# Expert stage of a decoder trunk: token rows scattered to slots and block results fetched back through DRAM

## The chip, the cores and the metric

One core of a Trainium2 chip runs the whole kernel. It has TensorE (matrix products into PSUM), VectorE, ScalarE, GpSimd and SyncE, and 16 DMA engines that move data between DRAM and SBUF. The metric is the device time in microseconds; the figure for a kernel is the median of its runs. Profiles come from one execution.

## The reference, cut to what matters

Two layers over 256 tokens of width 1024. The change concerns the last part: a mixture of 8 SwiGLU experts, two per token, then the gated residual add and the final RMSNorm.

```python
logits = (hf @ router_w + router_b).astype(jnp.float32)
probs = jax.nn.softmax(logits, axis=-1)
top_p, top_i = lax.top_k(probs, TOP_K)            # TOP_K = 2
top_p = top_p / jnp.sum(top_p, axis=-1, keepdims=True)
...
for e in range(N_EXPERTS):                         # 8
    out = out + gates[:, e:e + 1] * _swiglu(hf, w_gate[e], w_up[e], w_down[e])   # 1024 -> 3584 -> 1024
...
x = x + gate_from_c * out                          # adaLN: shift, scale and gate come from c
return _rmsnorm_f32(x, final_norm_g)
```

Everything is float32.

## The kernel before

**Order of the work.** Attention and convolution, the dense feed-forward, the state-space layer and its GLU, the router, and then the expert stage. The activations lie with channels on the partitions and tokens along the free dimension (`buf_b` is `B`, the residual `x`; `H` the normed input).

**Blocks and slots.** Each token takes two slots, one for each expert chosen. Slots are grouped in blocks of 32 (`BLK`); an expert has at least two blocks (`LEAST`) and the whole at most 28 (`MOST`, 896 slots). In this run there are 22: 2, 6, 3, 2, 2, 2, 3 and 2 for experts 0 to 7. The router's counts give `items`, the running number of blocks, which every engine loads into registers as `upto`. VectorE works out `slot_of[0]` and `slot_of[1]`, the two slots of each token.

**Gather.** A group of 128 slots (four blocks) is gathered by matrix products: `sel` holds, for each token and slot, 1 where the slot is the token's, and `gather(g)` (L724) multiplies the token-major copy `h_tm` of `H` with it. ScalarE copies the result into `hg` (`take_gathered`). `GATHER_AT` says before which expert a group is gathered in round 0: groups 0 and 1 before expert 0, 2 and 3 before expert 1, 4, 5 and 6 before experts 2, 4 and 6.

**Rounds.** The hidden width of 3584 is cut in 7 rounds (`ROUNDS`) of 512. Within a round the experts come in order, and within an expert its blocks. GpSimd copies a block's columns into `hbuf` (L1602); TensorE makes gate and up (`gate_up`, L744: 32 products) into PSUM, ScalarE the SiLU (L1010), VectorE the product and the transpose (L1052, L1470); TensorE makes the down product of the block before (`e_down`, L753: 16 products) between two blocks' gate and up; VectorE adds it to `acc` (`keep`). Each product is two instructions in the trace.

**Weights.** Each expert and round takes three pairs of ring slots of 2 MiB (`expert_stream`; two for gate and up, one for down), 168 in all. SyncE issues them in order. Seven pair slots lie in the ring; two more (`more`) join at pair 24 (`MORE_AT`), since until then `more` holds `h_tm`, `sel`, `places` and `spread`. A pair's load waits until the last block that uses its slot is done.

**Scatter and end.** In the last round the finished block goes through `keep_last` and `gate_rows` (three VectorE operations that make the block's row of gate weights per token from `reps`) and `scatter` (L762: 8 products over four row groups), which adds it into PSUM over all tokens. `spread_turn` (L734) and the copy into `reps` prepare that in round 0. After the last block: `residual`, then the final norm by channel: squares on ScalarE, `sums` (L417) on TensorE, root, reciprocal, eight products on VectorE, four stores of `out` (L1037) from ScalarE's queue.

## Time and profile before

| what | value |
|---|---|
| runs shown | 1510.95 us median of 3 (1510.21 to 1512.93) |
| span of the profiled execution | 1512.1 us, slowest (only) core |
| TensorE, VectorE, ScalarE, GpSimd busy | 1430.2, 370.1, 159.2, 137.5 us |
| mean granted TensorE clock | 0.985 |
| DRAM traffic | 478.10 MB read, 13.63 MB written |
| expert stage | from 606.5 us to the end of the span |

The profiled execution's own time is given as its span, 1.15 us above the median of the runs. An engine's busy time is the time in which at least one of its instructions runs; a matmul's end is modelled, so a busy TensorE needn't be at its peak. In the slices each digit or number stands for a fortieth of the span, 37.8 us. In a row of the timeline the first number is the start and the second the time that the merged instructions take; what stands in brackets is how long the engine was idle before and what released it.

### The profile page before, as it was taken

The page shows a single profiled execution, that of the slowest core. Times are in us where ns is not written, and L with a number is a line of the kernel's source. Part 1 is how long each engine was busy: PE and PEld are TensorE (multiplying, and loading weights), DVE is VectorE, ACT ScalarE, POOL GpSimd, SP SyncE. Part 2 cuts the span into 40 slices and gives each one's busy share as a digit, 9 for nine tenths or more (in the row PEclk, how much of TensorE's full clock was granted, in tenths as well). Part 3 has the DMA queues.
Part 4 walks back from the last instruction along what each step waited for, and adds up shares of the span by engine and source line. Part 5 has one row for each costly group of instructions (what it writes and reads, how often), then busy time and mean ns, then how long its engine had stood idle before and what let it go on. Part 6 is the DMA issues. An engine that isn't in the chain of part 4 may idle for free.

```text
span 1512.1 us, 44722 instructions
## 1 busy us (share of the span) xinstructions
PE 1430.2 (95%) x19890; PEld 1062.4 (70%) x19890; DVE 370.1 (24%) x1021; ACT 159.2 (11%) x378; POOL 137.5 (9%) x230
## 2 busy tenths in 40 slices
PE   4999999999998898999999989989989989999996
PEld 3887888888887787666567757767757755555554
DVE  2816230220203715111111111111111111113334
ACT  2103111101112203100000000000000000000001
POOL 0000043140300000000000000000000000000000
PEclk8999999999999999999999999999999999999999
DMA  9948595646328705759999999999999999999870
GB/s 385 422 165 333 194 372 216 262 188 247 140 84 356 313 0 232 326 193 426 426 421 410 426 426 395 426 426 408 427 425 407 424 427 405 413 426 394 361 308 29
DMA packets 44202, 493.91 MB, mean 327 GB/s; under 512 B 4896, under 2 KB 5152, under 8 KB 5792
## 3 DMA queue, kind: packets, MB, share of 16 engines
q1 hardware_dynamic: 41040, 475.02, 76.4%
q10 hardware_dynamic: 3024, 16.73, 2.7%
q8 instruction: 125, 2.05, 0.5%
q14 instruction: 13, 0.11, 0.0%
HBM read 478.10 MB, written 13.63 MB: 325 GB/s over the span
## 4 chain that ended last, share of the span: by engine, by line
PE 82%; DMA 12%; DVE 4%; ACT 1%; issue 1%; SPq 0%; POOL 0%; DVEq 0%; POOLq 0%
PE PS L744 30%; PE PS L443 20%; PE PS L753 15%; DMA ring<-in_expert_stream 9%; PE PS L598 5%; PE PS L427 2%; DMA arena<-in_expert_stream 2%; DMA ring<-in_dense_stream 2%; PE PS L762 2%; PE PS L724 1%; DVE arena L1052 1%; PE PS L652 1%; PE PS L568 1%; PE PS L580 1%; PE PS L475 1%; PE PS L417 1%
## 5 line engine op out<-in xcount | busy, mean ns | idle before, releaser
L744 PE MATMUL PS<-ring,arena 128*32 128x256 f32 x7040 | 405.4, 381 | 21.7 <-DMA ring<-in_expert_stream 13.1
L744 PEld LDWEIGHTS PS<-ring,arena 128*32 128x32 f32 x7040 | 251.5, 110 | 154.1 <-issue 16.9
L443 PE MATMUL PS<-arena,ring 128*128 128x256 f32 x1408 | 314.2, 384 | 4.3 <-ACT arena L855 2.7
L443 PEld LDWEIGHTS PS<-arena,ring 128*128 128x128 f32 x1408 | 269.9, 193 | 44.5 <-issue 6.3
L753 PE MATMUL PS<-ring,arena 128*32 128x256 f32 x4928 | 298.4, 381 | 0.8 <-DVE consts L1052 0.8
L753 PEld LDWEIGHTS PS<-ring,arena 128*32 128x32 f32 x4928 | 178.6, 111 | 91.4 <-issue 4.4
L744 PE MATMUL PS<-arena 128*32 128x256 f32 x2816 | 162.9, 382 | 10.7 <-DMA arena<-in_expert_stream 7.8
L1052 DVE TENSOR_TENSOR stat<-stat,PS 128x128 f32<-128x128 f32 x154 | 44.4, 288 | 505.3 <-ACT stat L1010 505.3
L1052 DVE TENSOR_TENSOR arena<-arena,PS 128x256 f32 (+1 forms) x123 | 55.3, 449 | 376.3 <-PE PS L443 236.5
L744 PEld LDWEIGHTS PS<-arena 128*32 128x32 f32 x2816 | 101.2, 111 | 63.9 <-DMA arena<-in_expert_stream 9.0
L1602 POOL COPY arena<-arena 128x256 f32 x153 | 61.3, 401 | 817.3 <-PE PS L744 768.8
L1010 ACT ACTIVATE stat<-PS 128x128 f32<-128x128 f32 x154 | 42.8, 278 | 806.5 <-PE PS L744 806.5
L598 PE MATMUL PS<-arena,ring 128*128 128x256 f32 x352 | 78.0, 381 | 0.0
L829 ACT ACTIVATE arena<-PS 128x512 f32<-128x512 f32 (+4 forms) x87 | 47.6, 560 | 263.4 <-PE PS L443 63.2
L598 PEld LDWEIGHTS PS<-arena,ring 128*128 128x128 f32 x352 | 66.6, 190 | 9.0 <-issue 0.4
L427 PE MATMUL PS<-ring,arena 128*32 128x128 f32 x1536 | 49.3, 283 | 16.4 <-DMA consts<-in_consts 10.7
L1052 DVE TENSOR_TENSOR arena<-arena 128x32 f32<-128x32 f32 (+9 forms) x158 | 61.1, 412 | 11.1 <-ACT arena L829 6.6
L427 PEld LDWEIGHTS PS<-ring,arena 128*32 128x32 f32 x1536 | 42.5, 114 | 23.8 <-DMA consts<-in_consts 10.7
L1470 DVE STREAM_TRANSPOSE arena<-stat 128x128 f32<-128x128 f32 x154 | 46.9, 305 | 23.7 <-PE PS L753 23.7
L762 PE MATMUL PS<-consts 32*128 32x256 f32 x384 | 27.5, 400 | 1.9 <-DVE consts L1052 1.9
L724 PEld LDWEIGHTS PS<-arena 128*128 128x128 f32 x224 | 25.5, 192 | 4.0 <-issue 3.1
L724 PE MATMUL PS<-arena 128*128 128x128 f32 x224 | 26.6, 278 | 1.5 <-DVE arena L1449 1.5
(187 smaller groups left out, 603.4 us busy)
## 6 DMA issues: line engine op xcount, KB each, us to landing
ring<-in_expert_stream SPq DMA_DIRECT2D x136, 2048.0 KB, 19.9
ring<-in_dense_stream SPq DMA_DIRECT2D x105, 1024.0 KB, 7.8
arena<-in_expert_stream SPq DMA_DIRECT2D x32, 2048.0 KB, 23.2
ssm_scratch<-arena ACTq DMA_DIRECT2D x12, 1024.0 KB, 5.0
ring<-ssm_scratch SPq DMA_DIRECT2D x12, 1024.0 KB, 9.8
arena<-in_xt ACTq DMA_DIRECT2D x1, 1024.0 KB, 13.9
arena<-in_ssm_small ACTq DMA_DIRECT2D x1, 1024.0 KB, 9.1
out_t<-arena ACTq DMA_DIRECT2D x4, 256.0 KB, 2.6
```

Of the source, the lines that this page charges most:

```text
L427: mm = pe.matmul(to[32 * q:32 * q + 32], cond[:, 32 * (4 * h + c):32 * (4 * h + c) + 32], w[:, c, q, :], start=(h == 0 and c == 0), stop=( ...
L443: mm = pe.matmul(PS[:, bank, j * T:(j + 1) * T], w[:, c, j * P:(j + 1) * P], moving[:, c, :], start=(c == 0), stop=(c == NC - 1))
L598: mm = pe.matmul(PS[:, 4 + n // 2, (n % 2) * T:(n % 2 + 1) * T], w[:, j * D + n * P:j * D + (n + 1) * P], f_hid[:, (f % 2) * 512 + j * T:( ...
L724: mm = pe.matmul(PS[:, bank + c // 4, (c % 4) * SLOT:(c % 4 + 1) * SLOT], h_tm[:, tt * D + c * P:tt * D + (c + 1) * P], sel[:, tt * MOST * ...
L744: mm = pe.matmul(PS[32 * q:32 * q + 32, 0, 0:256], hbuf[:, c * BLK:(c + 1) * BLK], w[:, q * 256:(q + 1) * 256], start=(c == 0), stop=(c == ...
L753: mm = pe.matmul(PS[32 * q:32 * q + 32, 1, 0:256], hidT[:, ch * BLK:(ch + 1) * BLK], w[:, q * 256:(q + 1) * 256], start=(ch == 0), stop=(c ...
L762: mm = pe.matmul(PS[:, 4 + q, h * T:(h + 1) * T], accb[rows, h * P:(h + 1) * P], gtb[rows, :], start=(first and h == 0), stop=last, skip_g ...
L829: return act.activation(out_ap, in_ap, ACT.Copy)
L1010: return act.activation(e_act_b, PS[:, 0, 0:SLOT], ACT.Silu)
L1052: return dve.tensor_tensor(o_, a, b, op)
L1470: return dve.transpose(hidT, e_hid_b)
L1602: return pool.tensor_copy(hbuf, hg[:, bass.ds(j * 256, 256)])
```

## The change

- **Slots through DRAM.** A DRAM tensor `row_scr` of 896 rows of 1024 is filled with rows of the input early on (ScalarE's queue, start of the dense feed-forward). GpSimd scatters the token rows of `h_tm` to their slots with four indirect DMAs (two halves of the tokens, two choices; 128 rows of 4 KiB each). When all four have landed (`rows_sent`), ScalarE issues a load of 128 rows into `hg` for each of the groups 1 to 6. TensorE turns each with eight transposes (`turn_rows`), and ScalarE copies it in place. Only group 0 is still gathered by products (`gather_first`). Group 1 is turned after block 0's gate and up.
- **`MORE_AT`** goes from 24 to 7: the two extra pair slots are used from pair 7 on, as soon as the first gather is done and the rows are sent.
- **No scatter by products.** In the last round VectorE finishes `acc` and multiplies the block by the gate from c laid out along the row (`gf_quads`, made in round 1 by `gate_row`); ScalarE stores the block to `row_scr` (`store_block`). After the last store GpSimd fetches, with four indirect DMAs, the two rows of each token. The residual is turned to token-major by 16 transposes (`turn_resid`), VectorE adds the two rows with their weights, and the final norm is made by token: square with its sum and root on ScalarE, reciprocal and scaling on VectorE, with the gain broadcast to all partitions. The host code undoes the other layout.

The core of the diff:

```diff
 PIECE = 2048
 W_IN, W_OUT, SSM, GLU = 12, 4, 3 * BATCHES, 8
-MORE, MORE_AT = 2, EXPERTS * STEP
+MORE, MORE_AT = 2, RING // 2
...
                 if prior is None:
-                    sp.wait_ge(e_gather, GATHERS)
-                    sp.wait_ge(spread_psum, 1)
+                    sp.wait_ge(e_gather, 1)
+                    sp.wait_ge(rows_sent, 16 * 4)
...
+            def gather_first():
+
+                pe.wait_ge(sel_ready, 1)
+                for c in range(NC):
...
+            def turn_rows(g):
+
+                pe.wait_ge(rows_back[g - 1], 16)
                 if g >= 2:
                     pe.wait_ge(hg_ready, g - 1)
                 bank = 6 - 2 * (g % 2)
                 for c in range(NC):
-                    for tt in range(2):
-                        mm = pe.matmul(PS[:, bank + c // 4, (c % 4) * SLOT:(c % 4 + 1) * SLOT],
-                                       h_tm[:, tt * D + c * P:tt * D + (c + 1) * P],
-                                       sel[:, tt * MOST * BLK + g * SLOT:tt * MOST * BLK + (g + 1) * SLOT], start=(tt == 0), stop=(tt == 1))
+                    mm = pe.transpose(PS[:, bank + c // 4, (c % 4) * SLOT:(c % 4 + 1) * SLOT],
+                                      hg[:, g * 1024 + c * P:g * 1024 + (c + 1) * P], ident)
                 mm.then_inc(e_gather, 1)
...
+            def gate_row():
+
+                pe.wait_ge(diag_ready, 1)
+                for c in range(NC):
+                    mm = pe.matmul(PS[:, 2 + c // 4, (c % 4) * P:(c % 4 + 1) * P], ones, g_diag[:, c * P:(c + 1) * P], start=True, stop=True)
+                mm.then_inc(gf_psum, 1)
 
...
+            for n in range(-(-MOST * BLK // T)):
+                rows = min(T, MOST * BLK - n * T)
+                act.dma_start(row_scr[n * T:n * T + rows, :], xt_in.rearrange("p (h d) -> (p h) d", d=D)[0:rows, :]).then_inc(rows_filled, 16)
...
             take_gathered(0)
-            take_gathered(1)
+            act.wait_ge(rows_sent, 16 * 4)
+            for g in range(1, GATHERS):
+                act.dma_start(hg[:, g * 1024:(g + 1) * 1024], row_scr[g * SLOT:(g + 1) * SLOT, :]).then_inc(rows_back[g - 1], 16)
...
                     silu().then_inc(silu_ready, 1)
+                    for g in range(1, GATHERED[0]):
+                        take_gathered(g)
...
+            def store_block(j):
+
+                act.wait_ge(y_scaled, j + 1)
+                act.dma_start(row_scr[bass.ds(j * BLK, BLK), :].rearrange("i (q n) -> q i n", q=4),
+                              acc[:, bass.ds(j * 256, 256)]).then_inc(y_stored, 16)
+
+            act.wait_ge(rows_filled, 16 * -(-MOST * BLK // T))
+            act.wait_ge(gu_done, upto[-1] * (ROUNDS - 1) + 1)
+            silu().then_inc(silu_ready, 1)
+            with act.Fori(1, upto[-1]) as j:
+                act.wait_ge(gu_done, j + upto[-1] * (ROUNDS - 1) + 1)
+                silu().then_inc(silu_ready, 1)
+                store_block(j - 1)
+            store_block(upto[-1] - 1)
+
+            act.wait_ge(down_done, upto[-1] * ROUNDS)
+            act.dma_start(gain_row, gain_in.partition_broadcast(P).rearrange("p o d -> p (o d)")).then_inc(gain_loaded, 16)
+            for tt in range(2):
+                act.wait_ge(mixed_ready, tt + 1)
+                act.activation(rows_sq, y_mix[tt], ACT.Square, accum_out=row_sum[:, tt:tt + 1]).then_inc(sum_ready, 1)
+                act.wait_ge(sum_ready, tt + 1)
+                act.activation(row_rms[:, tt:tt + 1], row_sum[:, tt:tt + 1], ACT.Sqrt, scale=1.0 / D,
+                               bias=consts[:, C_EPS:C_EPS + 1]).then_inc(root_ready, 1)
+            for tt in range(2):
+                for h in range(2):
+                    at = slice(tt * D + h * 512, tt * D + (h + 1) * 512)
+                    act.wait_ge(final_ready, 2 * tt + h + 1)
+                    act.dma_start(out[:, at], ring[:, FINAL + at.start:FINAL + at.stop]).then_inc(out_stored, 16)
...
+            for k in range(2):
+                s = dve.tensor_copy(slots_i[:, 2 * k:2 * k + 2], slot_of[k])
+            s.then_inc(slots_ready, 1)
+            for t_ in range(2):
+                s = dve.tensor_scalar(sel[:, t_ * SLOT:(t_ + 1) * SLOT], iota, slot_of[0][:, t_:t_ + 1], None, ALU.is_equal)
+            link(s)
+            for t_ in range(2):
+                part_of = sel[:, t_ * SLOT:(t_ + 1) * SLOT]
+                s = dve.scalar_tensor_tensor(part_of, iota, slot_of[1][:, t_:t_ + 1], part_of, ALU.is_equal, ALU.add)
+            s.then_inc(sel_ready, 1)
...
+            def scale_block(j):
+
+                dve.wait_ge(acc_done, blocks * (ROUNDS - 1) + j + 2)
+                tt(wide_block(acc, j), wide_block(acc, j), gf_quads, ALU.mult).then_inc(y_scaled, 1)
...
+                if rnd == 1:
+                    dve.wait_ge(gf_psum, 1)
+                    for q in range(4):
+                        s = dve.tensor_copy(gf_quads[32 * q:32 * q + 32], PS[32 * q:32 * q + 32, 2 + q // 2, q % 2 * 256:(q % 2 + 1) * 256])
+                    link(s)
...
-                    if rnd < ROUNDS - 1:
-                        keep(wide_block(acc, j - 1), rnd).then_inc(acc_done, 1)
+                    keep(wide_block(acc, j - 1), rnd).then_inc(acc_done, 1)
                     dve.wait_ge(e_hid, j + blocks * rnd + 1)
                     turn_hid().then_inc(hidT_ready, 1)
                     if rnd == ROUNDS - 1:
-                        dve.wait_ge(e_scat, j + 1)
-                        keep_last(j - 1)
-                        dve.wait_ge(gt_ready, j)
-                        gate_rows(j - 1)
+                        scale_block(j - 1)
...
+            dve.wait_ge(x_turned, 1)
+            for t_ in range(2):
+                dve.wait_ge(y_back[t_], 16)
+                link(dve.scalar_tensor_tensor(y_mix[t_], y_rows[2 * t_], r2[6][:, t_:t_ + 1],
+                                              PS[:, 4 + 2 * t_:6 + 2 * t_, :].rearrange("p b n -> p (b n)"), ALU.mult, ALU.add))
+                dve.wait_ge(y_back[2 + t_], 16)
+                dve.scalar_tensor_tensor(y_mix[t_], y_rows[2 * t_ + 1], r2[7][:, t_:t_ + 1], y_mix[t_], ALU.mult,
+                                         ALU.add).then_inc(mixed_ready, 1)
+            dve.wait_ge(mixed_ready, 2)
+            dve.wait_ge(gain_loaded, 16)
+            for t_ in range(2):
+                dve.wait_ge(root_ready, t_ + 1)
+                link(dve.reciprocal(row_rms[:, t_:t_ + 1], row_rms[:, t_:t_ + 1]))
                 for h in range(2):
-                    s = residual(3, 2 * q + h, PS[:, 4 + q, h * T:(h + 1) * T])
-                s.then_inc(e_x, 1)
-
-            inv_rms(4)
-            for c in range(NC):
-                dve.scalar_tensor_tensor(H[:, c, :], B[:, c, :], gain(4)[:, c:c + 1], stat[:, :], ALU.mult,
-                                         ALU.mult).then_inc(final_ready, 1)
+                    at = slice(h * 512, (h + 1) * 512)
+                    dve.scalar_tensor_tensor(ring[:, FINAL + t_ * D + h * 512:FINAL + t_ * D + (h + 1) * 512], y_mix[t_][:, at],
+                                             row_rms[:, t_:t_ + 1], gain_row[:, at], ALU.mult, ALU.mult).then_inc(final_ready, 1)
...
+            pool.wait_ge(rows_filled, 16 * -(-MOST * BLK // T))
+            pool.wait_ge(htm_ready, 4)
+            pool.wait_ge(slots_ready, 1)
+            for t_ in range(2):
+                for k in range(2):
+                    pool.indirect_dma_start(out=row_scr[:, :], out_offset=bass.IndirectOffsetOnAxis(ap=slots_i[:, 2 * k + t_:2 * k + t_ + 1], axis=0),
+                                            in_=h_tm[:, t_ * D:(t_ + 1) * D], in_offset=None).then_inc(rows_sent, 16)
...
+            pool.wait_ge(down_done, upto[-1] * ROUNDS)
+            pool.wait_ge(y_stored, upto[-1] * 16)
+            pool.sem_inc(y_all, 1)
+            pool.wait_ge(y_all, 1)
+            pool.wait_ge(slots_ready, 1)
+            for t_ in range(2):
+                for k in range(2):
+                    pool.indirect_dma_start(out=y_rows[2 * t_ + k], out_offset=None, in_=row_scr[:, :],
+                                            in_offset=bass.IndirectOffsetOnAxis(ap=slots_i[:, 2 * k + t_:2 * k + t_ + 1], axis=0)
+                                            ).then_inc(y_back[2 * k + t_], 16)
```

## Rows read from the trace of the kernel before

**Rows 1.** the page: busy time (share of the span), and what the 40 slices moved
```profile
PE 1430.2 (95%) x19890; PEld 1062.4 (70%) x19890; DVE 370.1 (24%) x1021; ACT 159.2 (11%) x378; POOL 137.5 (9%) x230
...
GB/s 385 422 165 333 194 372 216 262 188 247 140 84 356 313 0 232 326 193 426 426 421 410 426 426 395 426 426 408 427 425 407 424 427 405 413 426 394 361 308 29
```

**Rows 2.** TensorE in order of time at the turn of rounds 0 and 1: start, us
```profile
742.46 3.64 PE L744 MATMUL PS<-ring,arena 128*32 128x256 f32 x64
745.91 1.91 PE L753 MATMUL PS<-ring,arena 128*32 128x256 f32 x32
747.64 3.64 PE L744 MATMUL PS<-arena 128*32 128x256 f32 x64
```

**Rows 3.** groups of instructions: busy us, mean ns, idle before
```profile
L1010 ACT ACTIVATE stat<-PS 128x128 f32<-128x128 f32 x154 | 42.8, 278 | 806.5 <-PE PS L744 806.5
...
L762 PE MATMUL PS<-consts 32*128 32x256 f32 x384 | 27.5, 400 | 1.9 <-DVE consts L1052 1.9
```

**Rows 4.** windows; us, busy (count) of PE, PEld, DVE, ACT, POOL; clock, DMA share, GB/s
```profile
864.00:984.00 120.00, 113.11 (x2089) 80.37 (x2084) 20.19 (x65) 5.84 (x21) 8.41 (x21) 1.00 0.99 417
...
1104.00:1224.00 120.00, 115.96 (x2116) 82.47 (x2112) 20.48 (x66) 6.11 (x22) 8.81 (x22) 0.99 1.00 419
```

**Rows 5.** waits of TensorE: us in total, times, longest
```profile
PE PS L744 <- DMA ring<-in_expert_stream: 16.0, 11, 2.7
...
PE PS L744 <- DMA arena<-in_expert_stream: 7.8, 2, 3.9
```

**Rows 6.** windows (columns as in group 4)
```profile
640.00:655.00 15.00, 15.00 (x284) 9.10 (x280) 2.69 (x9) 0.55 (x2) 0.92 (x3) 1.00 0.00 0
660.00:680.00 20.00, 18.19 (x321) 11.09 (x324) 2.80 (x9) 2.69 (x5) 1.60 (x4) 1.00 0.76 288
1460.00:1470.00 10.00, 10.00 (x184) 5.90 (x180) 3.05 (x9) 0.56 (x2) 0.80 (x2) 1.00 0.37 157
1507.00:1510.00 3.00, 0.00 (x0) 0.00 (x0) 1.48 (x4) 0.00 (x0) 0.00 (x0) 0.50 0.95 333
36.00:44.00 8.00, 8.00 (x36) 6.94 (x35) 6.28 (x25) 4.51 (x7) 0.00 (x0) 0.92 1.01 425
1002.00:1006.00 4.00, 3.71 (x44) 1.99 (x48) 0.29 (x1) 0.28 (x1) 0.40 (x1) 0.66 1.00 426
```

**Rows 7.** TensorE in order of time at the end
```profile
1491.42 1.93 PE L753 MATMUL PS<-ring,arena 128*32 128x256 f32 x32 [0.76 <-DVE consts L1052]
```

**Rows 8.** all engines in order of time where the stage starts
```profile
596.11 0.17 DVE L1436 TENSOR_REDUCE arena<-arena 128x2 f32<-128x16 f32 x1
...
606.49 3.66 PE L744 MATMUL PS<-ring,arena 128*32 128x256 f32 x64 [0.56 <-issue]
...
610.95 3.66 PE L744 MATMUL PS<-ring,arena 128*32 128x256 f32 x64 [0.80 <-DVE stat L1052]
...
625.50 3.66 PE L744 MATMUL PS<-ring,arena 128*32 128x256 f32 x64 [1.82 <-POOL arena L1602]
```

**Rows 9.** landings of SyncE's pairs issued at 582.8 to 587.3, then at 911.9
```profile
DMA to landing us min/median/max: 8.9/20.6/33.9
...
DMA to landing us min/median/max: 9.4/11.7/14.0
```

**Rows 10.** DMA packets and issues: count, KB each, median us to landing
```profile
DMA packets 44202, 493.91 MB, mean 327 GB/s; under 512 B 4896, under 2 KB 5152, under 8 KB 5792
...
out_t<-arena ACTq DMA_DIRECT2D x4, 256.0 KB, 2.6
...
arena<-in_positions ACTq DMA_DIRECT2D x1, 128.0 KB, 8.5
```

**Rows 11.** the eight transposes of the spread
```profile
L734 PE MATMUL PS<-consts,arena x8: 272/273/328, 678.0 to 678.9; 128*128 128x128 f32 x8
```

**Rows 12.** VectorE groups by shape
```profile
L1052 DVE TENSOR_TENSOR arena<-arena 128x512 f32<-128x512 f32 x36 | 23.8, 688 | 7.3 <-ACT arena L829 6.6
...
L1052 DVE TENSOR_TENSOR arena<-arena,buf_b 128x1024 f32<-128x1024 f32 x8 | 9.8, 1225 | 0.3
```

More of the change, by code:

```diff
@@ L248, in trunk_kernel @@
         hg = arena[:, 0:MOST * 256]
-        h_tm, sel, places, spread = more[:, 0:2048], more[:, 2048:3840], more[:, 3840:4736], more[:, 4736:5760]
+        h_tm, sel = more[:, 0:2048], more[:, 2048:2304]
         o = 0
@@ L755, in e_down, with turn_resid @@
                 mm.then_inc(down_done, 1)
-            def scatter(first=False, last=False):
-                for h in range(2):
-                    for q in range(4):
-                        rows = slice(BLK * q, BLK * q + BLK)
-                        mm = pe.matmul(PS[:, 4 + q, h * T:(h + 1) * T], accb[rows, h * P:(h + 1) * P], gtb[rows, :],
-                                       start=(first and h == 0), stop=last, skip_group_check=True)
-                mm.then_inc(e_scat, 1)
+            def turn_resid():
+                for tt in range(2):
+                    for c in range(NC):
+                        mm = pe.transpose(PS[:, 4 + 2 * tt + c // 4, (c % 4) * P:(c % 4 + 1) * P], B[:, c, tt * P:(tt + 1) * P], ident)
+                mm.then_inc(x_turned, 1)
             spin(3, 3)
             pe.wait_ge(htm_ready, 4)
-            gather(0)
+            gather_first()
             pe.wait_ge(items_ready, 1)
-            upto = blocks_upto(pe, range(EXPERTS // 2))
-            gather(1)
-            upto += blocks_upto(pe, range(EXPERTS // 2, EXPERTS))
+            upto = blocks_upto(pe)
             for rnd in range(ROUNDS):
-                if rnd == ROUNDS - 1:
-                    pe.wait_ge(part_zeroed, 1)
-                    pe.wait_ge(reps_ready, 1)
-                    scatter(first=True)
+                if rnd == 1:
+                    gate_row()
                 for e in range(EXPERTS):
@@ L812, in _ @@
             e_down(expert_at(ROUNDS - 1, EXPERTS - 1))
-            pe.wait_ge(gt_ready, upto[-1])
-            scatter()
-            pe.wait_ge(gt_ready, upto[-1] + 1)
-            pe.wait_ge(acc_done, upto[-1] * ROUNDS + 1)
-            scatter(last=True)
-            spin(3, 2)
-            sums(4, 0)
+            pe.wait_ge(hg_ready, GATHERS)
+            turn_resid()
         @block.scalar
@@ L1024, in _ @@
                     silu().then_inc(silu_ready, 1)
+                    for g in range(1, GATHERED[0]):
+                        take_gathered(g)
                 with act.Fori(upto[e - 1] if e else 1, upto[e]) as j:
@@ L1027, in _ @@
                     silu().then_inc(silu_ready, 1)
-            for rnd in range(1, ROUNDS):
+            for rnd in range(1, ROUNDS - 1):
                 with act.Fori(0, upto[-1]) as j:
```

126 lines of the change are left out of this document (42 added, 84 removed).

## The prediction

> **What bounds the kernel now.** I read the page first: TensorE is busy 95% of the span [rows 1]. The slices then split it: from slice 18 on (counted from 0, each 37.8 us) the DMA engines move about 426 GB/s as well, with dips, until the last three; slices 16 and 17, where the expert stage begins, show 326 and 193 GB/s [rows 1]. So TensorE and the weight stream are close to each other there. A block costs TensorE 3.46 us of gate and up and 1.73 us of down (the distances between starts), 5.18 us from block to block [rows 2]. 154 such blocks (as many as the stage's SiLUs [rows 3], 7 rounds of 22) are 798 us. The weights are 168 pairs of 2 MiB; at 427 GB/s a pair takes 4.9 us, and over whole rounds, at 417 to 419 GB/s, 5.0 us, so a round of 24 pairs takes 120 us, against 114 us of TensorE [rows 4]. The waits agree: TensorE waits for the expert stream some 24 us in all [rows 5], mostly in rounds 1 to 5. These are paced by DMA. Round 0 isn't: at 640 to 655 us the DMA engines stand still [rows 6], because all seven pair slots are full while expert 1's six blocks run (625.5 to 656). The last round isn't either: each block there also carries a scatter on TensorE, 1.2 us with its gap (384 matmuls are 22 scatters and two more [rows 3]), and the stream ends at about 1463.7 us, since 1460 to 1470 moves 157 of 427 GB/s [rows 6]. TensorE ends its last down product at 1493.4 [rows 7], 18.7 us before the end of the span.
>
> The question is then what sets the stream's end after the change, and what must follow it.
>
> **Front of the stage.** The slots are known at 596.3 us, and gate/up of block 0 starts at 606.5, behind two gathers [rows 8]. After the change one stands before it: some 3 us earlier, 603.5. But block 1 may start only when group 1 has come back from DRAM (hg_ready). ScalarE waits for all four scatters (rows_sent) before it issues the six row loads, and its first SiLU and the copies of groups 1 to 3 are queued behind; SyncE's pairs 7 and 8, and all pairs behind them, wait for the scatters too. The upper bound is hardly more, 627: the 7 pairs' and the scatters' own work, since no new pair is issued meanwhile. I take 624.6, the mechanism of the nearest row.
>
> The first row load then shares the engines with pairs 7 and 8: 8 x 0.76 = 6.1 us from 626, landing at 633.5. TensorE has been idle since 607. After an idle 2.4 us before 1002.3 the granted clock is 0.66 over the next 4 us [rows 6], so it wakes at 1.2 of its 2.4 GHz: 2.2 us for eight transposes that take 1.1 now [rows 11], 1.2 for the copy on ScalarE, 0.5 on GpSimd: block 1 at 637.5, and 2 us more in it for the clock, against 610.9 now [rows 8]. Block 1 with the down product (7.2), turns of groups 2 and 3, two copies and GpSimd's, together some 4.3 (2.2 of turns, 1.2 of the last copy, 0.5, waits): **expert 1 starts at 649 in place of 625.5**. Turns of 1.1 us in place of gathers of 3.8 give back 3 x 2.75 and the spread's 1.1, 9.4 us of TensorE in round 0, but the stream is the bound behind it, so they go into slack. The two extra slots let the stream hold nine pairs, three experts, instead of seven. It resumes when expert 1's last gate/up ends, 649 + 5 x 5.18 + 3.46 = 678.4, with pair 12; a pair on an idle queue lands 9.4 us after issue [rows 9], 687.8. 155 more pairs at 5.0 us are 775 us, with one gap of 3.7 us (expert 2 releases its slot only at 697): **the stream ends at 1466.5**, 3 us later than now. So the 24 us lost at the front are nearly paid by the two slots, which remove the second stall (288 GB/s at 660 to 680 us [rows 6]).
>
> **Last round.** The scatter goes, 27 us of TensorE that lay over the stream's pace. Expert 1's second gate/up pair lands 19 pairs before the end, at 1371.5; then half a gate/up and a down (3.5), 19 blocks (98.4), the last down (2.4), 2 for the clock: last down at **1478**, 15 us earlier than now. Scaling is one VectorE operation of 0.4 where four stood; gate/up hides it. The gain row (8 matmuls, 4 copies in round 1) is hidden by the 6 us a round in which TensorE waits for the stream. The fill of `row_scr`, 3.5 MiB on ScalarE's queue at the start of the dense feed-forward, is hidden by the 14 pieces that SyncE keeps ahead (without that cover 8.6 us).
>
> The 22 block stores of 128 KiB are the unknown. All DMAs of this trace run on 16 engines: the 4,896 packets under 512 B are the completions of 306 transfers [rows 10], and all of these have 128 rows or a multiple outermost. The new store's DRAM side has 4 outermost, with 32 rows of 1 KiB under each. No row has such a transfer. Spread as before, an engine gets 8 KiB of a store; split by the outer count, 4 engines get 32 KiB each. At 333 GB/s, the rate of the small rows of the final store [rows 6], that is 0.39 or 1.56 us per store, 8.6 or 34.3 us in all (27 at the stream's rate). I take four: 16 equal shares of 128 rows look like a split of the outermost dimension, and 4 can't be split in 16. Those engines carry the stream as well and are full through the round, so the work adds: 1466.5 + 34.3 + 1.9 of receipt = **1502.7** until the last store has landed, though TensorE ends near 1481 (one store row of 0.05 us behind each stream row of 0.61 slows the last 14 pairs or so by some 8%, of which 3 us reach TensorE).
>
> The Trainium skill, "DMA: Bandwidth & Descriptors", section "Why a DMA increments its semaphore by 16 and not by 1", says that a DMA takes the largest number of engines up to 16 that divides the slowest dimension of both sides, which is 4 here. By it the sum would be the one taken; were it not so, the first rival. No row here shows it.
>
> **Tail.** GpSimd gathers 4 x 512 KiB: the first lands after 3.4 us (2.6 for 256 KiB [rows 10], 0.6 more data, 0.2 to start), the others 1.2 each behind it, the fourth at +7.7 with its issue. No row has GpSimd issuing a DMA. Bounds: hidden behind the data, or each transfer only after the one before, 14 us; I take the first, as SyncE's and ScalarE's transfers queue. Last mix on VectorE 1.3, square on ScalarE 1.1, root 0.5, reciprocal 0.2, two halves of 0.75 (0.69 for 128x512 and 1.22 for 128x1024 [rows 12], a little for the link), store 2.7: **15.2**, up to 21.5. Sum 1517.9 against the span of 1512.1. The span lies 1.15 us above the median of the runs shown (1510.95), so 1516.7.
>
> **Rivals.**
> - *The stores use 16 engines.* Stream ends at 1475, last down 1483, last store landed 1487, end 1502, time 1501: faster. It decides from about 24 us of store work on the busiest engine downward. For it: all 306 transfers of this trace. Against: the shape of the access. That TensorE's freed 27 us simply show (1496) is its limit with costless stores.
> - *The scatter isn't held up by the stream.* Landed by 605, expert 1 at 624, all behind it 25 us earlier: end 1493, time 1492. Against: the positions load.
> - *GpSimd's gathers run one after the other.* Tail 21.5: time 1523. The front hardly changes, bounded by 627. Nothing for or against.
>
> **Chances.** Forecast 0.50, with a range of its own of 1506 to 1527 (store work 27 to 41 us, row landings 4 us either way); serial gathers 0.12; 16 engines 0.24; quick scatter 0.14. A measurement tells 0.2%, 3 us, from no change. Of the forecast's share about a seventh lies below 1508 and 0.15 of all within 3 us of now: faster 0.43, same 0.15, slower 0.42. The range 1488 to 1530 leaves out less than 2 in 10.
>
> **What would show it.** TensorE idle from about 607 to 633; the scatter landing near 624; DMA engines still at about 655 to 678; expert 1 from 649; rounds 1 to 5 of 120 us; last down near 1480; then 20 us in which a quarter of the DMA engines work, before the gathers. It is wrong if stores land within 5 us of issue, if the scatter lands before 612, or if a DMA issue on ScalarE holds up its SiLU, which would stall TensorE in the last round.

## Result: 1.6% slower, outside the predicted range

| | before | after |
|---|---|---|
| median of 4 runs each, us | 1510.8 | 1535.4 |
| lowest and highest, us | 1510.2 and 1512.9 | 1526.9 and 1542.3 |
| profiled execution's span, us | 1512.1 | 1538.0 |

The ratio is 1.0162, 95% interval 1.0124 to 1.02. The prediction had 1516.7 with a range of 1488 to 1530: the direction was the forecast one (with a chance of 0.42), the size four times as large.

The page of the changed kernel, against [rows 1] (busy time; then the slices of 38.5 us: granted clock in tenths, and GB/s). TensorE's busy time fell by 29 us, and yet the span grew by 26. That 29 lies near the scatter's 27.5 [rows 3] is chance: some 16 us of gathers, less the turns in their place, went as well, and products at a lower granted clock took longer, 9 us of them in the last round (see below):

```profile
PE 1401.4 (91%) x19364; PEld 1041.4 (68%) x19364; DVE 344.5 (22%) x952; ACT 158.0 (10%) x378; POOL 142.6 (9%) x229
...
PEclk9999999999999999699999999999999999999887
...
GB/s 386 422 147 364 198 408 223 281 208 197 136 115 378 247 1 333 370 203 386 426 398 412 425 428 414 427 427 410 426 425 406 427 426 413 427 426 356 407 203 111
```

Counted from 0, the clock digits 8 and 8 of slices 37 and 38 and the 356 and 203 GB/s of slices 36 and 38 belong to the last round. The 7 of slice 39 is mostly the tail: that slice starts at 1499.5, and the round's end still runs at 1.00. I went there after the front of the stage, since the forecast has separate terms for the two.

**Front.** All engines in order of time, at the turn from block 0 to block 1 and to expert 1 (against [rows 8]):

```profile
626.41 2.99 ACTq L1023 DMA_DIRECT2D arena<-row_scratch  x6
626.45 0.83 SPq L388 DMA_DIRECT2D arena<-in_expert_stream  x2
629.44 0.28 ACT L1016 ACTIVATE stat<-PS 128x128 f32<-128x128 f32 x1 [24.37 <-issue]
...
634.98 1.97 PE L746 MATMUL PS<-consts,arena 128*128 128x128 f32 x8 [23.18 <-DMA arena<-row_scratch]
...
638.80 6.37 PE L764 MATMUL PS<-ring,arena 128*32 128x256 f32 x64 [1.85 <-POOL arena L1628]
...
650.66 1.72 PE L764 MATMUL PS<-ring,arena 128*32 128x256 f32 x28 [1.86 <-POOL arena L1628]
```

Both queues that wait for the scatters start at 626.4, 28 us after GpSimd issued the first one (598.26). TensorE waits 23.2 us for the first group of rows. Expert 1 starts at 650.7, against 625.5 before.

**Rounds 1 to 5.** Windows, with the columns of group 4 (the first of them in round 0, against [rows 6]):

```profile
655.00:678.00 23.00, 23.00 (x432) 13.90 (x428) 4.37 (x14) 1.11 (x4) 1.61 (x4) 1.00 0.33 126
...
900.00:1020.00 120.00, 115.92 (x2108) 82.43 (x2112) 19.82 (x64) 6.14 (x22) 8.88 (x22) 0.99 1.00 422
1140.00:1260.00 120.00, 116.10 (x2116) 82.13 (x2112) 20.46 (x66) 6.13 (x22) 8.85 (x22) 0.99 1.00 420
```

The stream pauses (126 GB/s) while expert 1's blocks run, and then paces the rounds at 120 us as before. The last round starts at 1359.0, with the gate/up whose SiLU is the 133rd of 154.

**Last round.** TensorE's and ScalarE's waits over the whole execution (us in total, times, longest):

```profile
ACT stat L1016 <- issue: 65.7, 4, 24.4
PE PS L764 <- DVE stat L1082: 12.9, 2, 9.3
...
PE PS L764 <- issue: 9.5, 2, 9.3
```

The SiLU (L1016) is late four times: once at the front (24.4 us, the row loads that stand before it in ScalarE's program), and three times, 41.3 us together, in the last round. ScalarE in order of time shows why. The second number of an ACTq line is the time that the issue of a DMA took:

```profile
1399.31 6.17 ACTq L1043 DMA_DIRECT2D row_scratch<-arena  x1
1405.83 0.28 ACT L1016 ACTIVATE stat<-PS 128x128 f32<-128x128 f32 x1 [9.32 <-issue]
1407.55 0.58 ACTq L1043 DMA_DIRECT2D row_scratch<-arena  x1
...
1442.10 12.01 ACTq L1043 DMA_DIRECT2D row_scratch<-arena  x1
1454.46 0.28 ACT L1016 ACTIVATE stat<-PS 128x128 f32<-128x128 f32 x1 [15.17 <-issue]
1456.19 15.05 ACTq L1043 DMA_DIRECT2D row_scratch<-arena  x1
1471.60 0.28 ACT L1016 ACTIVATE stat<-PS 128x128 f32<-128x128 f32 x1 [16.85 <-issue]
```

A block's store is usually issued in 0.58 us. Three issues take 6.2, 12.0 and 15.1 us: ScalarE is held in them, and the next block's SiLU comes right after, late. TensorE in order of time over the same stretch:

```profile
1401.16 1.90 PE L773 MATMUL PS<-ring,arena 128*32 128x256 f32 x32
1406.57 6.48 PE L764 MATMUL PS<-ring,arena 128*32 128x256 f32 x64 [3.52 <-DVE stat L1082]
...
1443.94 1.92 PE L773 MATMUL PS<-ring,arena 128*32 128x256 f32 x32
1455.21 6.06 PE L764 MATMUL PS<-ring,arena 128*32 128x256 f32 x64 [9.35 <-DVE stat L1082]
...
1472.29 3.64 PE L764 MATMUL PS<-ring,arena 128*32 128x256 f32 x32 [9.30 <-issue]
```

Each late SiLU stops TensorE: 3.5, 9.4 and 9.3 us, 22.2 in all. Behind each stop a block's gate/up (64 instructions) takes 6.1 to 6.5 us in place of 3.6. The granted clock over these three stretches is 0.55 to 0.59 (1.00 between the stops), so for most of the time the lower of its two levels, 1.2 of 2.4 GHz. The stream stops too, since its slots come free only as TensorE uses them. Windows:

```profile
1400.00:1420.00 20.00, 16.48 (x257) 9.38 (x249) 2.67 (x9) 0.83 (x3) 1.21 (x3) 0.83 0.73 288
...
1440.00:1460.00 20.00, 10.65 (x160) 5.99 (x152) 2.09 (x7) 0.28 (x1) 0.40 (x1) 0.75 1.01 431
1460.00:1480.00 20.00, 10.70 (x156) 5.99 (x152) 1.43 (x5) 0.56 (x2) 0.81 (x2) 0.74 0.68 270
```

The clock column (0.83, 0.75, 0.74) and the GB/s column (288, 270) show both. At 1440 to 1460 the stream still runs at 431 GB/s while TensorE is busy for half of the time: it is filling the slots. So it isn't the stream that is late.

**Tail.** The end in order of time, against [rows 7]:

```profile
1512.04 1.93 PE L773 MATMUL PS<-ring,arena 128*32 128x256 f32 x32 [0.89 <-DVE arena L1497]
...
1520.37 1.00 POOL L1650 DMA_INDIRECT ring<-row_scratch,slots_i  x1 [15.53 <-issue]
...
1524.91 1.28 DVE L1545 SCALAR_TENSOR_TENSOR ring<-ring,arena,PS 128x1024 f32<-128x1024 f32 x1 [9.98 <-DMA ring<-row_scratch,slots_i]
...
1530.20 1.28 DVE L1548 SCALAR_TENSOR_TENSOR ring<-ring,arena 128x1024 f32<-128x1024 f32 x1
...
1532.71 2.32 ACTq L1067 DMA_DIRECT2D out_t<-ring  x4
```

The last down product ends at 1514.0 (1493.4 before). The gathers start 6.4 us later, when the last stores have landed, and the end follows 17.6 us behind them.

### The profile page after: what moved, and what is told of

Same layout as the page of the kernel before. It is cut to its first block, busy times and chain, and to the rows that moved or that the text cites. A ratio compares the mean times of both kernels' runs of the same rounds, so it can differ in the third digit from the quotient of the medians.

```text
span 1538.0 us, 43659 instructions
## 1 busy us (share of the span) xinstructions
PE 1401.4 (91%) x19364; PEld 1041.4 (68%) x19364; DVE 344.5 (22%) x952; ACT 158.0 (10%) x378; POOL 142.6 (9%) x229
## 2 busy tenths in 40 slices
DMA packets 49391, 508.28 MB, mean 330 GB/s; under 512 B 5288, under 2 KB 8360, under 8 KB 10920
## 4 chain that ended last, share of the span: by engine, by line
PE 79%; DMA 13%; DVE 3%; issue 1%; ACTq 1%; ACT 1%; POOL 0%; SPq 0%; POOLq 0%; DVEq 0%
PE PS L764 30%; PE PS L456 20%; PE PS L773 15%; DMA ring<-in_expert_stream 5%; PE PS L611 5%; DMA arena<-in_expert_stream 3%; PE PS L440 2%; DMA ring<-in_dense_stream 2%; DMA row_scratch<-arena,slots_i 2%; DVE arena L1082 1%; ACTq L1043 1%; PE PS L581 1%; PE PS L665 1%; PE PS L593 1%; PE PS L488 1%
## 5 line engine op out<-in xcount | busy, mean ns | idle before, releaser
L1082 DVE TENSOR_TENSOR arena<-arena,PS 128x256 f32 (+1 forms) x145 | 64.5, 445 | 403.8 <-PE PS L456 238.6
L1016 ACT ACTIVATE stat<-PS 128x128 f32<-128x128 f32 x154 | 42.8, 278 | 838.8 <-PE PS L764 773.1
L764 PE MATMUL PS<-arena 128*32 128x256 f32 x1568 | 96.9, 386 | 5.2 <-DMA arena<-in_expert_stream 5.2
L773 PE MATMUL PS<-arena 128*32 128x256 f32 x1568 | 95.1, 381 | 0.0
L764 PEld LDWEIGHTS PS<-arena 128*32 128x32 f32 x1568 | 58.5, 112 | 34.1 <-DMA arena<-in_expert_stream 6.2
L773 PEld LDWEIGHTS PS<-arena 128*32 128x32 f32 x1568 | 58.2, 111 | 27.4 <-issue 1.0
L746 PE MATMUL PS<-consts,arena 128*128 128x128 f32 x48 | 7.2, 303 | 23.2 <-DMA arena<-row_scratch 23.2
## 6 DMA issues: line engine op xcount, KB each, us to landing
arena<-in_xt ACTq DMA_DIRECT2D x1, 1024.0 KB, 13.9
```

Source lines behind the costliest of these rows:

```text
L764: mm = pe.matmul(PS[32 * q:32 * q + 32, 0, 0:256], hbuf[:, c * BLK:(c + 1) * BLK], w[:, q * 256:(q + 1) * 256], start=(c == 0), stop=(c == ...
L773: mm = pe.matmul(PS[32 * q:32 * q + 32, 1, 0:256], hidT[:, ch * BLK:(ch + 1) * BLK], w[:, q * 256:(q + 1) * 256], start=(ch == 0), stop=(c ...
L1016: return act.activation(e_act_b, PS[:, 0, 0:SLOT], ACT.Silu)
L1082: return dve.tensor_tensor(o_, a, b, op)
```

## The experiments

The theory from this profile: a block store reaches only four DMA engines, so its rows pile up in ScalarE's queue; when too many are outstanding the issue is held, the SiLU behind it is late, and TensorE and the stream stop. Besides that, the front loses some 20 us because the scatters stand behind seven pairs. The main rival: the stores cost nothing special, and the front's delay accounts for the loss by itself.

All profiled executions side by side. The last round is the time from its first gate/up to the end of the last down product; the late column adds up TensorE's waits in it for a SiLU (in the run with stores from GpSimd, for the copy into `hbuf`):

| run | expert 1 starts | last round starts | last round | late | ratio to before, interval |
|---|---|---|---|---|---|
| before | 625.5 | 1349.4 | 143.9 | 0 | |
| the change | 650.7 | 1359.0 | 155.0 | 22.2 | 1.0162, 1.0124 to 1.02 |
| rows outermost | 644.3 | 1354.7 | 125.0 | 0 | 0.9976, 0.996 to 0.9992 |
| no stores | 646.2 | 1354.7 | 123.3 | 0 | 0.9959, 0.9941 to 0.9978 |
| pairs held | 631.0 | 1342.0 | 148.2 | 18.8 | 1.004, 1.0017 to 1.0063 |
| four stores | 651.0 | 1366.1 | 123.2 | 0.2 | 0.9986, 0.9968 to 1.0004 |
| pairs held, four stores | 630.8 | 1343.0 | 124.6 | 0.4 | 0.9874, 0.9841 to 0.9908 |
| pairs held, rows outermost | 627.4 | 1339.3 | 125.4 | 0 | 0.9883, 0.9843 to 0.9923 |
| half the bytes | 645.0 | 1355.4 | 146.7 | 15.1 | 1.0134, 1.0098 to 1.017 |
| from GpSimd | 648.1 | 1358.4 | 165.4 | 28.4 | 1.0299, 1.0263 to 1.0336 |
| eight outermost | 649.0 | 1360.7 | 144.6 | 13.9 | 1.0095, 1.0064 to 1.0125 |
| two outermost | 649.3 | 1357.8 | 175.9 | 46.9 | 1.0335, 1.0295 to 1.0374 |

Single executions differ by up to 6.5 us before the stage's first block (it starts between 602.0 and 608.5), so the length of the last round is the firmer measure, and the ratios rest on 2 to 10 runs each.

**1. The store with 128 rows outermost.**

```diff
-act.dma_start(row_scr[bass.ds(j * BLK, BLK), :].rearrange("i (q n) -> q i n", q=4),
+act.dma_start(row_scr[bass.ds(j * BLK, BLK), :].rearrange("i (q n) -> (i q) n", q=4),
```

> The store of a finished block keeps its bytes, its place on ScalarE's queue and its one issue, but its DRAM side has 128 rows outermost in place of 4; the four quarters of a slot's row are thereby mixed up, so the output's values are not the reference's. Theory A (the stores run on 4 of 16 DMA engines, one 1 KiB row behind each 16 KiB row of the stream, fill ScalarE's queue, and the blocked issue holds up the SiLU): no issue above 1 us, no idle of TensorE behind it in the last round, last down product near 1488 us in place of 1514, last store within 5 us of it, time about 1513 us, 23 us less than the changed kernel. Theory B (the loss in the last round is store traffic as such, or VectorE's extra step): blocked issues or waits of the same size stay and the time stays within 8 us of 1535.

Measured: 1507.2 us, last down product at 1479.7. The page's packets, a store's landing, and ScalarE's queue (q10) over 1380 to 1400 us:

```profile
DMA packets 49655, 508.28 MB, mean 339 GB/s; under 512 B 5552, under 2 KB 8624, under 8 KB 11184
```

```profile
DMA to landing us min/median/max: 1.7/10.5/11.1
```

```profile
q10 hardware_dynamic: 505, 0.47, 6.7%
```

The same bytes in as many 1 KiB rows from the same engine, and nothing is held: each issue takes about 0.35 us, and the last round is 30 us shorter. The small packets count the engines. A transfer ends with one on each engine that it used; the changed kernel has 5288 under 512 B, this one 5552, which is 22 x 12 more: 16 engines in place of 4 for each of 22 stores. The run without stores has 5201, 87 fewer than the change, which is four a store but for one.

**2. No block stores.** The gathers wait for `down_done` and `y_scaled` instead and read what the rows held before, so the expert part of the output is left out.

```diff
 def store_block(j):
     act.wait_ge(y_scaled, j + 1)
-    act.dma_start(row_scr[...], acc[:, bass.ds(j * 256, 256)]).then_inc(y_stored, 16)
...
-pool.wait_ge(y_stored, upto[-1] * 16)
+pool.wait_ge(y_scaled, upto[-1])
```

> Leaves out the 22 block stores, so the fetched rows are not the results; everything else stays, the gathers wait for the last scaled block. Gives the price of the stores in all. Theory A: as the run with rows outermost, less their 4 to 8 us: last down product near 1484, time about 1505 us. Theory B (VectorE's step): last down product stays near 1514.

Measured: 1506.2 us, last down product at 1477.95. The forecast's 1478 for a last round without the stores' load was right. Beside run 1 it says that stores on 16 engines cost next to nothing (1507.2): the 29 us between this and the change are the price of the stores as they are made. VectorE's scaling step stays in this run, so theory B is out.

**3. The pairs held back.** SyncE issues only three pairs before the scatters.

```diff
 for n in range(RING // 2):
...
+    if n == STEP:
+        sp.wait_ge(rows_sent, 16 * 4)
     load_pair(n)
```

> SyncE waits for the scattered rows before it issues expert pair 3, so that the scatter and the row loads find the DMA engines nearly free. Theory A (the scatter is held up by the 7 pairs before it): rows sent near 605 us in place of 626, block 1 near 617 in place of 639, expert 1 near 630 in place of 651, and the 20 us reach the end: time about 1515 us. Theory B (the stream is the bound and loses what the scatter gains, since four pairs start 20 us later): expert 1 earlier, but the stream resumes no earlier or TensorE waits for pairs in round 0, time within 5 us of 1535.

Measured: 1517.6 us. ScalarE issues the row loads at 604.8 in place of 626.4, expert 1 starts at 631.0 and the last round at 1342.0, 17 us earlier than in the change. So the front's delay isn't absorbed by the two extra slots. But the last round still takes 148.2 us, with the issue held for up to 14.8 us: the two costs are separate, and the rival, one cost alone, is out.

**4. Four stores a block,** each of one quarter with its 32 partitions.

```diff
-act.dma_start(row_scr[...].rearrange("i (q n) -> q i n", q=4), acc[:, bass.ds(j * 256, 256)]).then_inc(y_stored, 16)
+for q in range(4):
+    act.dma_start(row_scr[bass.ds(j * BLK, BLK), q * 256:(q + 1) * 256],
+                  acc[BLK * q:BLK * q + BLK, bass.ds(j * 256, 256)]).then_inc(y_stored, 16)
...
-pool.wait_ge(y_stored, upto[-1] * 16)
+pool.wait_ge(y_stored, upto[-1] * 64)
```

> Each block store is four DMAs of 32 rows of 1 KiB from ScalarE's queue, each with 32 rows outermost, so that it can use 16 engines. Same result as the changed kernel. Theory A: as the run with rows outermost but for three more issues a block, 1 to 2 us on ScalarE, which may delay a SiLU by some tenths: time about 1515 us. Theory B: as the changed kernel, 1535, or more for the issues.

Measured: 1509.0 us, with the same numbers in the same places of DRAM. A window of the last round: TensorE busy throughout, at full clock, with the stream at 423 GB/s.

```profile
1440.00:1460.00 20.00, 20.00 (x376) 14.63 (x372) 4.47 (x15) 1.11 (x4) 1.60 (x4) 1.00 1.01 423
```

The four issues take ScalarE 1.87 us a block in place of 0.58, a few of them up to 2.87, and TensorE waits 0.2 us for that in the whole round.

**5. Both cures,** and **6. the hold with rows outermost.** The edits are those of runs 3 and 4, and of 3 and 1.

> Both cures at once: SyncE issues its pairs from the third expert step on only after the scattered rows are in DRAM, and each block goes out as four stores of 32 partitions. If the two costs are separate (scattered rows queued behind weight rows in front, ScalarE's issue held in the last round), the two gains add: the last round starts near 1338.5 (where it started with the hold alone; 1355.5 in the changed kernel) and takes the 120 to 123 us that it took with four stores, so the last down product ends near 1462, the span near 1486, the time 1480 to 1492, ratio to before 0.98 to 0.988. Rival: the stream sets the end of the last round in either case and the stores' bytes delay it by as much as the hold won; then the last down product stays near 1480 and the time near 1502, no better than four stores alone.

> The hold with one store a block whose 128 rows stand in one outermost dimension (the block's columns land in another order, so this gives times only): as the run with both cures, but with 22 issues instead of 88. Last down product near 1460, time 1480 to 1490. If four issues a block cost ScalarE or the chip's queues something, it is up to 5 us faster than the four stores; if only the spread over engines counts, the two agree within 3 us.

Measured: 1491.9 and 1492.7 us, the second above its expected 1480 to 1490. The gains add: 17.8 us by the hold alone and 26.4 by the four stores alone make 44.2, and both together give 43.5. The 1338.5 and 1355.5 in the expectation were misread from the traces: each is the second half of the gate/up before. The last round starts at 1342.0 with the hold alone, 1359.0 in the change, and 1343.0 in run 5. It takes 124.6 us, and the last down product ends at 1467.6, 6 us later than expected. The two forms of the store agree within 1 us: the spread over engines counts, the number of issues doesn't. With run 5 the exchange through DRAM is 1.3% faster than the kernel before. In it the scatters land in 4.4 us instead of 19.3 (medians of the four; the last to land took 4.7 us at most instead of 24.1), and TensorE waits 3.2 us for the first group of rows instead of 23.2; the landing of the four scatters and TensorE in order of time:

```profile
DMA to landing us min/median/max: 4.3/4.4/4.7
```

```profile
615.54 1.09 PE L748 MATMUL PS<-consts,arena 128*128 128x128 f32 x8 [3.19 <-DMA arena<-row_scratch]
618.47 6.37 PE L766 MATMUL PS<-ring,arena 128*32 128x256 f32 x64 [1.84 <-POOL arena L1631]
```

**7. Rows or bytes.** The changed kernel's stores with 512-byte rows; half of each block is left out.

```diff
-act.dma_start(row_scr[...].rearrange("i (q n) -> q i n", q=4), acc[:, bass.ds(j * 256, 256)])
+act.dma_start(row_scr[...].rearrange("i (q n) -> q i n", q=4)[:, :, 0:128], acc[:, bass.ds(j * 256, 128)])
```

> The changed kernel with the stores' rows cut from 1 KiB to 512 bytes (half of each block is left out), as many rows on the same four engines. If what fills ScalarE's queue is the number of rows, each passed behind one 16 KiB row of the stream, nothing changes: issues held 6 to 15 us, TensorE stalled by some 20 us in the last round, last down product near 1510, time 1525 to 1540. Rival, the bytes: half the backlog, stalls under 8 us together, last down product under 1495, time near 1515.

Measured: 1529.4 us, waits of 15.1 us, last down product at 1502.1. ScalarE's queue passes 140 packets in 1380 to 1400 us, against 139 in the change, with half the bytes, and the fifth store is the first to be held in both. So rows, not bytes, set how fast the queue passes and when the first issue is held. The stalls are a third shorter all the same, and the last down product is 8 us earlier than the row count alone was to give; why, no run shows.

**8. The stores from GpSimd,** each behind a copy into `hbuf` and one block later.

```diff
 with pool.Fori(2, upto[-1]) as j:
     pool.wait_ge(gu_done, j + upto[-1] * (ROUNDS - 1))
     load_block(j).then_inc(hbuf_ready, 1)
+    pool.wait_ge(y_scaled, j - 1)
+    pool.dma_start(row_scr[...block j - 2...].rearrange("i (q n) -> q i n", q=4), acc[...]).then_inc(y_stored, 16)
```

> The changed kernel with the same 128-partition stores issued by GpSimd, each behind its copy into hbuf and one block later. If the loss is the wait of SiLU behind a held issue on ScalarE, SiLU is never late here: no TensorE wait on SiLU in the last round, and the last down product ends near 1481 to 1490, as the prediction had it. Should GpSimd's queue fill too, its copy into hbuf is late in SiLU's place, and TensorE waits for that by a like amount (last down near 1510). Rival: four busy engines slow the stream itself, whoever issues; then TensorE waits on the stream in the last round and ends near 1505 or later with no late SiLU and no late copy.

Measured: 1555.2 us. The case that the expectation named second came about, and worse than it said (1523.8 for the last down product, 1510 expected): the SiLU isn't late, the copy is. TensorE's and GpSimd's waits in 1355 to 1525 us:

```profile
POOL row_scratch L1641 <- issue: 88.1, 13, 9.9
...
PE PS L764 <- POOL arena L1621: 28.4, 7, 5.6
...
PE PS L764 <- DMA ring<-in_expert_stream: 3.4, 2, 2.3
```

Here too the engine that issues the stores is held, and what stands behind them in its program is late. But it isn't the same transfer. By its page beside that of the run without stores, each store is 32 packets of 2 to 8 KB and 96 under 512 B beside 16 completions, in place of 128 of 1 KiB and four completions. And while the issue is held, from 1383.8 to 1394.8 us, the queue passes 144 packets, just one store's: GpSimd has about one store outstanding where ScalarE's queue had over 300 packets. So this run shows that moving the issue doesn't help, not that one limit holds both engines. TensorE's waits for the stream are 3.4 us here and 4.4 in the change, in both cases at the start of the round: four loaded engines don't slow the stream enough for TensorE to notice.

**9 and 10. Eight and two slices outermost,** 16 and 64 rows in each.

```diff
-act.dma_start(row_scr[...].rearrange("i (q n) -> q i n", q=4), ...
+act.dma_start(row_scr[...].rearrange("i (q n) -> (i q) n", q=4).rearrange("(b a) n -> a b n", a=8), ...   # a=2 in run 10
```

> The changed kernel's stores with 8 slices in the outermost dimension of the DRAM side in place of 4 (16 rows in each; the block's rows land in another order, so times only). If the engines that serve a store are as many as its outermost dimension has slices, it goes over 8: 16 rows an engine and block in place of 32. With one row passed for each stream row of 0.61 us, 9 a block of 5.4 us, 7 rows an engine are left behind by each block in place of 23, so ScalarE's issue is held late in the round or not at all: TensorE's waits on SiLU in the last round together under 6 us (22 with four), last down product 1480 to 1488, time 1507 to 1520, packets under 512 B 5288 + 22 x 4. Rival: the spread isn't what counts and only the full 16 cures it; then waits and time as in the changed kernel (1530).

> The same with 2 slices outermost (64 rows in each, times only). By the same theory two engines serve each store, 64 rows an engine and block, and 55 of them are left behind by each block while the stream runs: ScalarE's issue is held from the third or fourth store on, TensorE stands still for most of the last round, the last down product ends beyond 1560 (1514 with four), packets under 512 B 5288 - 22 x 2. Rival as before: no difference from the changed kernel (1514, 1530 in all).

Measured: 1527.6 and 1559.3 us, with 13.9 and 46.9 us of waits (22.2 with four slices, none with 128). The packets and ScalarE's queue over 1380 to 1400 us, with eight:

```profile
DMA packets 49479, 508.28 MB, mean 333 GB/s; under 512 B 5376, under 2 KB 8448, under 8 KB 11008
...
q10 hardware_dynamic: 277, 0.27, 3.8%
```

and with two:

```profile
DMA packets 49347, 508.28 MB, mean 326 GB/s; under 512 B 5244, under 2 KB 8316, under 8 KB 10876
...
q10 hardware_dynamic: 68, 0.07, 1.0%
```

5376 and 5244 are 5288 + 88 and 5288 - 44, as expected: eight and two engines. The queue's packets follow: 68, 139 and 277 over two, four and eight engines, 34 or 35 an engine each time. I missed the size with eight: under 6 us of waits and 1507 to 1520 us expected, 13.9 and 1527.6 measured, since the issue was held from the 11th store on, five times for 6 to 8 us. I missed it the other way with two: the last down product was to end beyond 1560 and ended at 1533.7; the issue was held three times only (20.0, 14.6 and 20.4 us, at the third, ninth and thirteenth store). The backlog by engine was no guide. Taking the queue's packets up to the moment when the first held issue went through from those of the stores issued before it (128 rows and one packet more for each engine used) leaves some 325 outstanding with four engines (528 - 203), 319 with eight (1360 - 1041), but only 156 with two (260 - 104). By the same count the twelfth and thirteenth stores of the change went through with some 278 and 264 outstanding. What the limit is stays open.

## Why the prediction was wrong

**The step that failed** is the last round: "Those engines carry the stream as well and are full through the round, so the work adds", with TensorE ending "near 1481". The mechanism was half right. The stores do go over four engines and do pass one row behind each stream row. The queues in the change at 1380 to 1400 us (packets, MB, share; q1 is SyncE's, q10 ScalarE's):

```profile
q1 hardware_dynamic: 576, 8.37, 98.3%
q10 hardware_dynamic: 139, 0.14, 2.0%
```

0.14 MB in 1 KiB rows are some 34 rows on each of four engines, and 8.37 MB in 16 KiB rows are 32 on each of 16: one for one. What I took from that was only a slow landing after TensorE's end. But 32 rows come every 5.2 us and about 9 leave, so the queue grows, and I didn't ask how many rows it can take, nor what stands behind the issue on ScalarE. "If a DMA issue on ScalarE holds up its SiLU" stood among the things that would make the prediction wrong, without a place among the rivals, a price or a chance. It should have been the third rival at least: two numbers of the forecast itself (32 rows in, 9 out) call for it.

In its place: the last round took 155.0 us where the forecast had 125 and the run without stores 123.3. TensorE over the round, of that run and then of the change in four windows:

```profile
1354.70:1478.00 123.30, 118.50 (x2149) 83.37 (x2142) 27.57 (x89) 6.09 (x22) 8.42 (x21) 0.99 0.88 372
```

```profile
1358.95:1400.00 41.05, 36.65 (x624) 21.51 (x620) 7.75 (x25) 1.67 (x6) 2.42 (x6) 0.92 1.01 427
1400.00:1440.00 40.00, 36.48 (x628) 22.00 (x620) 7.61 (x25) 1.94 (x7) 2.82 (x7) 0.91 0.85 342
1440.00:1480.00 40.00, 21.35 (x308) 11.98 (x300) 3.53 (x12) 0.83 (x3) 1.21 (x3) 0.74 0.85 350
1480.00:1514.00 34.00, 33.11 (x613) 20.10 (x605) 8.37 (x27) 1.67 (x6) 2.02 (x5) 1.00 0.25 90
```

Busy it was for 127.6 us (the four windows added up) in place of 118.5, idle for 27.5 in place of 4.8. So of the 31.7 us about 22.7 are the stops and 9.1 the same products at the lower clock, which follows from the stops (the clock column). During the stops the four engines do catch up, so that the last store lands 6 us after the last down product and not 22 after it. All in all the stores were done at 1520.4, 17.7 us later than forecast (1502.7).

That the change came out slower, as forecast, was luck in part. The forecast's slowness lay in the 22 us between the last down product and the last landing, and they came to 6; the measured slowness lies in stops that it didn't price.

**The store's spread** was sized rightly: four engines. The Trainium skill, "DMA: Bandwidth & Descriptors", section "Why a DMA increments its semaphore by 16 and not by 1", gives the number of engines as the largest up to 16 that divides the slowest dimension of both sides; the packet counts of the change and of runs 1, 9 and 10 agree for 4, 16, 8 and 2.

**The front** came out within 2 us of each term: scatters in DRAM at 624.6 forecast and 626.4 measured, first turn 633.5 and 635.0, block 1 637.5 and 638.8, expert 1 649 and 650.7. Only block 0 missed, 603.5 and 606.5, because its gate/up follows the copies on ScalarE and GpSimd (4.2 us of wait) as well as the gather. Then the stream: the last round was to start at about 1356 by the same working and did at 1359.0. But "the 24 us lost at the front are nearly paid by the two slots" misread the account. It hides that the delay costs 16 to 17 us against what the change could be: runs 5 and 3 start the last round that much earlier with the same slots. What the slots bring by themselves no run shows, since none leaves them out.

**The rival with quick scatters** was given 1492 for a chip that passes small rows quickly. The chip doesn't, as the positions load said; run 5 gets 1491.9 by making way for them, with the stores mended too. That the two numbers agree is chance: the rival's sum kept the slow landing of the stores.

**The tail** was 17.6 us after the stores' landing, 15.2 forecast. The first gather took 4.5 us until VectorE could use it (3.4 forecast), and the last mix started 9.8 us after the first issue (7.7 forecast). GpSimd needs 0.94 to 1.0 us for each issue, 1.25 from one to the next. The gathers were not serial.

**The sum.** The span was forecast at 1517.9 and was 1538.0: 17.7 from the stores' end and 2.4 from the tail. Added up again, three of its terms are off by some tenths (32 rows of 0.76 us are 24.3 and not 24.5, the first row load lacks 0.5 of the receipt, and the tail's items make 15.0 and not 15.2); nothing turns on them.

## What to carry to other kernels

A DMA issue is not free of waiting: compare the rows that a store puts on its busiest engine per step with the rows that this engine passes beside the stream in that step, and if more go in than out, price what stands behind the issue on the issuing engine. Give the outermost dimension of both sides of a DMA a multiple of 16, or split the transfer so that each part has one; here that alone was worth 1.7%. And where small rows must get through, hold the bulk stream's unneeded loads back until they have: three pairs in flight instead of seven turned a 19.3 us landing into 4.4.

## What the runs showed of the hardware that I had not expected

- The issue of a DMA was held for up to 15.1 us on ScalarE (20.4 with two engines), and GpSimd stood up to 9.9 us before its own. It didn't come evenly: in the change the fifth store was held, then the twelfth and the thirteenth, and the six between went out at 0.58 us each. A stop empties the queue: with TensorE's stop the stream pauses, and the stores' rows then have the engines to themselves. In 1405 to 1415 us ScalarE's queue passed 596 packets, all that was outstanding, beside 80 of the stream, and had to fill again before the next hold:

```profile
q1 hardware_dynamic: 80, 1.05, 30.7%
q10 hardware_dynamic: 596, 0.59, 16.7%
```

- SyncE's and ScalarE's queues, on an engine that they share, took turns row by row: 34 or 35 of ScalarE's packets an engine in 20 us beside 32 rows of 16 KiB, for rows of 1 KiB and of 512 bytes alike. The same page of the Trainium skill, section "Queues, rings and completion order", has an engine drain a packet of typically some 9 to 17 descriptors from one queue before it turns to the next. The trace doesn't agree: in each 0.6 us from 1388.0 to 1394.6 ScalarE's queue passed 3 to 6 rows on its four engines, mostly four, so one an engine beside each stream row of 0.61 us. With turns of nine rows or more, 5 us and more would go by between them. The measurement decides for this kernel.
- Single executions of one kernel spread by up to 20 us: 1526.9 to 1542.3 us for the change (4 runs), 1485.7 to 1499.9 for run 6 (5), 1510.3 to 1530.3 for run 9 (10), but 1490.6 to 1492.5 for run 5 (4). Why, no run here shows.
